# Feed-forward input projection by seven block products instead of eight, with block sums made on chip

## The reference

```python
    x = x + gt1 * (merged @ w_out)
    h2 = rmsnorm(x, g_norm[1]) * (1 + sc2) + sh2
    u, gg = jnp.split(h2 @ w_ffn_in, 2, axis=-1)
    x = x + gt2 * ((jax.nn.silu(gg) * u) @ w_ffn_out)
```

## Time and profile before

| what | value |
|---|---|
| median of 3 runs | 1094.04 us (1091.89 to 1094.91) |
| profiled execution, first to last instruction | 1095.1 us |
| PE busy | 1045.0 us (95%) |
| DVE, ACT, POOL busy | 395.5, 366.5, 368.7 us |
| feed-forward input stage, about | 676 to 948 us |

### The profile page before, as it was taken

The page is one execution under the profiler, slowest core; times in us unless marked ns, Lnnn a source line. Parts: engine busy times, 40 slices in busy tenths (PEclk is TensorE's granted clock), DMA queues, the critical chain, the costliest instruction groups (busy, mean ns, idle before and its releaser), DMA issues.

```text
span 1095.1 us, 25416 instructions
## 1 busy us (share of the span) xinstructions
PE 1045.0 (95%) x10988; PEld 966.9 (88%) x10988; DVE 395.5 (36%) x926; ACT 366.5 (33%) x745; POOL 368.7 (34%) x252
## 2 busy tenths in 40 slices
PE   6999999999998988989898999999999999999997
PEld 3899989999996766777787999999999999999997
DVE  4400000194045676566556576222222222200003
ACT  4443333353444444345232233322322232211112
POOL 2165433343316061401160333333343334344331
PEclk8899999999999999899998999999999999999999
DMA  9986666343311000020341532233222322132322
GB/s 358 352 276 235 234 206 198 99 139 119 113 42 36 18 7 22 13 82 3 131 130 43 198 116 58 77 92 99 77 77 83 107 78 65 55 104 79 92 67 82
DMA packets 118174, 122.23 MB, mean 112 GB/s; under 512 B 5396, under 2 KB 102848, under 8 KB 115656
## 3 DMA queue, kind: packets, MB, share of 16 engines
q1 hardware_dynamic: 112864, 111.86, 31.8%
q10 hardware_dynamic: 5224, 9.10, 2.5%
HBM read 108.33 MB, written 15.23 MB: 113 GB/s over the span
## 4 chain that ended last, share of the span: by engine, by line
PE 86%; DVE 7%; issue 3%; ACT 3%; POOL 1%; ACTq 1%; DVEq 0%; POOLq 0%
PE ps L1566 83%; PE ps L1917 2%; DVE s_sb L1306 1%; PE ps L1817 1%; POOL w_lo L595 1%; DVE s_sb L1340 1%; ACT x_sq L743 0%; DVE xn L1118 0%; DVE gring L1477 0%; DVE Pb L1277 0%; DVE y_sb L1549 0%; DVE mt L1479 0%; ACT mgh L1031 0%; DVE XX L1287 0%; ACTq L729 0%
## 5 line engine op out<-in xcount | busy, mean ns | idle before, releaser
L595 POOL TENSOR_TENSOR w_lo<-w_raw,w_hi 128x2048 fp32r<-128x2048 f32 (+1 forms) x66 | 282.3, 4277 | 564.0 <-ACT w_hi L753 544.9
L1566 PE MATMUL ps<-hh,w_hi 128*128 128x274 f32 x1376 | 290.0, 293 | 2.7 <-DVE hl L1128 2.0
L1566 PE MATMUL ps<-hh,w_lo 128*128 128x274 f32 x1376 | 288.1, 292 | 0.0
L1566 PE MATMUL ps<-hl,w_hi 128*128 128x274 f32 x1376 | 286.6, 291 | 0.0
L1566 PEld LDWEIGHTS ps<-hh,w_hi 128*128 128x128 f32 x1376 | 219.0, 190 | 12.8 <-issue 11.2
L1566 PEld LDWEIGHTS ps<-hh,w_lo 128*128 128x128 f32 x1376 | 218.7, 190 | 0.8 <-issue 0.8
L1566 PEld LDWEIGHTS ps<-hl,w_hi 128*128 128x128 f32 x1376 | 219.0, 190 | 0.0
L753 ACT ACTIVATE w_hi<-w_raw 128x2048 fp32r<-128x2048 f32 (+1 forms) x66 | 117.5, 1781 | 106.6 <-PE ps L1566 101.1
L1566 PE MATMUL ps<-ah,w_hi 128*128 128x274 f32 x352 | 75.3, 290 | 0.3 <-POOL w_lo L595 0.3
L1566 PE MATMUL ps<-ah,w_lo 128*128 128x274 f32 x352 | 75.4, 290 | 0.0
L1566 PE MATMUL ps<-al,w_hi 128*128 128x274 f32 x352 | 75.2, 290 | 0.0
(11 more groups left out here) (375 smaller groups left out, 1537.8 us busy)
## 6 DMA issues: line engine op xcount, KB each, us to landing
w_raw<-in_w_ffn_in SPq DMA_DIRECT2D x44, 512.0 KB, 4.6
w_raw<-in_w_in SPq DMA_DIRECT2D x42, 512.0 KB, 5.0
ada_l<-in_w_ada SPq DMA_DIRECT2D x16, 1024.0 KB, 6.4
ada_w<-in_w_ada SPq DMA_DIRECT2D x8, 1024.0 KB, 13.6
w_raw<-in_w_ffn_out SPq DMA_DIRECT2D x16, 384.0 KB, 4.0
w_raw<-in_w_ffn_out SPq DMA_DIRECT2D x16, 320.0 KB, 3.4
g_d<-gst SPq DMA_DIRECT2D x16, 274.0 KB, 2.4
gring<-g_d SPq DMA_DIRECT2D x16, 274.0 KB, 3.2
```

The costliest lines, as they stand in the source:

```text
L595: pool.tensor_tensor(w_lo[:, s, 0:cols], w_raw[:, s, 0:cols], w_hi[:, s, 0:cols].bitcast(F32), ALU.subtract).then_inc(lo_done, 1)
L1566: return pe.matmul(out, lhsT, rhs, start=start, stop=stop)
```

## The change

The first unit (U_UP) stays as it was. For the other 21 the unit is one 2 x 2 block product: rows are the gate's (A11, A12) and the up block (A21, A22) with even and odd k blocks as columns of A; B11, B12 are the two halves of the tokens for even k, B21, B22 for odd k. The Winograd form of Strassen's scheme makes it with seven products of 4 k blocks x 3 terms = 12 matmuls, 84 for a unit.

- Token sums t1 to t4 (`tq`, float32), 4 subtractions of 274 columns for each of the 4 pairs of k blocks, are made once on DVE in the loop of the output projection's residuals; ACT makes their high parts `th`, POOL their low parts `tl`, each in 4 operations of 4 x 274 columns.
- Weight sums s1 to s4 (`w_sum`, one buffer, 4 x 512 columns) are made for every unit on DVE.
- ACT and POOL make high and low parts of 7 x 512 columns a unit in 4 groups (1024, 1024, 512, 1024 columns), into one buffer `ws_hi`, `ws_lo`: a group is overwritten when its products of the unit before are done.
- A unit takes four PSUM banks, two sets in turn. Products 3, 5 and 6 are added to banks whose content ACT has copied before (`rest`, 4 copies of 274 columns); DVE adds bank and copy for each of the four quarters, then scales by `rstd2` (both operands in SBUF now).
- The activations are kept in float32 (`a_f`). Their high parts go to the memory of `hh`, `hl`, `th`, `tl` as these come free in the last unit; ACT makes them and DVE the low parts at the end of the stage (`act_high`, `act_low`), and PE's first output tile waits block by block.
- `w_raw` holds the two blocks one behind the other. Final norm buffers move.

```diff
-            two_by_two(sp, U_UP, NUP, up)
+            def up_later(i, s):
+                sp.wait_ge(wslo_done, i * NGR + (WSLO - (U_ST + 1) * NGR))
+                up_blocks(i, s)
...
+            def token_low(c):
+                pool.wait_ge(th_done, TH + c + 1)
+                pool.tensor_tensor(tl[:, :, c, :], tq[:, c % 2, :, :], th[:, :, c, :].bitcast(F32), ALU.subtract)\
+                    .then_inc(tl_done, 1)
...
+            def blocks_low(i, s):
+                for g, (a, z) in enumerate(FIRST_OF):
+                    pool.wait_ge(wshi_done, i * NGR + (WSHI + g + 1 - U_ST * NGR))
+                    of = blocks(a, z)
+                    pool.tensor_tensor(of(ws_lo), group_source(s, g), of(ws_hi).bitcast(F32), ALU.subtract)                        .then_inc(wslo_done, 1)
+            two_by_two(pool, U_ST, NST, blocks_low)
...
+            def blocks_high(i, s, g):
+                a, z = FIRST_OF[g]
+                if g in (0, 2):
+                    act.wait_ge(raw_in[s], i * 16 + (32 - 16 * s))
+                else:
+                    act.wait_ge(wsum_done, i * 4 + (WSUM + (3, 4)[g // 2] - U_ST * 4))
+                if isinstance(i, int) and i == U_ST:
+                    act.wait_ge(unit_mm, U_UP + (g >= 2))
+                else:
+                    act.wait_ge(prod_mm, i * NPR + (PROD + z - (U_ST + 1) * NPR))
+                act.activation(blocks(a, z)(ws_hi), group_source(s, g), ACT.Copy).then_inc(wshi_done, 1)
...
+            def up(i, s):
+                kept(i, s, 0)
+                blocks_high(i + 1, 1 - s, 0)
+                kept(i, s, 1)
+                kept(i, s, 2)
+                blocks_high(i + 1, 1 - s, 1)
+                kept(i, s, 3)
+                blocks_high(i + 1, 1 - s, 2)
+                gated_silu(i)
+                blocks_high(i + 1, 1 - s, 3)
...
+            def token_sums(c):
+                if c >= 2:
+                    dve.wait_ge(tl_done, TL + c - 1)
+                b11, b12, b21, b22 = [tmp_a[:, r, h * H:(h + 1) * H] for r in range(2) for h in range(2)]
+                t1, t2, t4, t3 = [tq[:, c % 2, b, :] for b in range(4)]
+                tt(t1, b12, b11, ALU.subtract).then_inc(tq_done, 1)
+                tt(t3, b12, b22, ALU.subtract).then_inc(tq_done, 1)
...
+                if j:
+                    token_sums(i)
...
+            def weight_sums(i, s):
+                dve.wait_ge(raw_in[s], i * 16 + (32 - 16 * s))
+                if not (isinstance(i, int) and i == U_ST):
+                    dve.wait_ge(wslo_done, i * NGR + (WSLO - U_ST * NGR))
+                a11, a12, a21, a22 = [raw_block(s, m, j) for m in range(2) for j in range(2)]
+                s1, s2, s4, s3 = [w_sum[:, b, :].rearrange("p (c m) -> p c m", m=P) for b in range(4)]
+                tt(s3, a21, a11, ALU.subtract).then_inc(wsum_done, 1)
+                tt(s1, a21, a22, ALU.add).then_inc(wsum_done, 1)
+                dve.wait_ge(wsum_done, i * 4 + (WSUM + 1 - U_ST * 4))
+                tt(s2, s3, a22, ALU.add).then_inc(wsum_done, 1)
+                dve.wait_ge(wsum_done, i * 4 + (WSUM + 3 - U_ST * 4))
+                tt(s4, a12, s2, ALU.subtract).then_inc(wsum_done, 1)
...
+            def quarter(i, s, n):
+                out, p, r, b = ((ff_g[:, 0:H], 1, 0, 1), (ff_g[:, H:W], 5, 2, 2), (ff_a[:, H:W], 6, 1, 0),
+                                (ff_a[:, 0:H], 6, 3, 0))[n]
+                dve.wait_ge(rest_ev, i * 4 + (REST + (1, 3, 2, 4)[n] - U_ST * 4))
+                dve.wait_ge(prod_mm, i * NPR + (PROD + p + 1 - U_ST * NPR))
+                tt(out, ps[:, 4 * (1 - s) + b, 0:H], rest[:, r, :], ALU.add).then_inc(quad_ev, 1)
+
+            def gate_up(i, s, between):
+                dve.wait_ge(act_f32, i - U_UP)
+                quarter(i, s, 0)
+                between()
+                quarter(i, s, 1)
+                dve.wait_ge(quad_ev, i * 4 + (QUAD + 10 - U_ST * 4))
+                tt(ff_g[:, :], ff_g[:, :], rstd2[:, :], ALU.mult).then_inc(ffg_f32, 1)
+                quarter(i, s, 2)
+                quarter(i, s, 3)
+                dve.wait_ge(quad_ev, i * 4 + (QUAD + 12 - U_ST * 4))
+                tt(ff_a[:, :], ff_a[:, :], rstd2[:, :], ALU.mult).then_inc(ffa_f32, 1)
+                dve.wait_ge(ffa_f32, i + (FFA + 1 - U_ST))
+                activated(i)
...
+            gate_up(U_DN - 1, (U_DN - 1) % 2, first_low)
+            for c in range(6, FT):
+                act_low(c)
...
+            def seven(i, s):
...
+                for p, (b, x) in enumerate(((0, b11), (1, b21), (2, t1), (0, t2), (3, t4), (2, b22), (0, t3))):
+                    if p in (0, 2, 4, 5):
+                        pe.wait_ge(wslo_done, i * NGR + (WSLO + GROUP_OF[p] + 1 - U_ST * NGR))
+                    if p == 0:
+                        pe.wait_ge(quad_ev, i * 4 + (QUAD + 4 - U_ST * 4))
+                    fresh = p in (0, 1, 2, 4)
+                    if not fresh:
+                        pe.wait_ge(rest_ev, i * 4 + (REST + {3: 1, 5: 2, 6: 3}[p] - U_ST * 4))
+                    xh, xl = x
+                    for c in range(HK):
+                        w = slice(block_column(p, c), block_column(p, c) + P)
+                        for j, (wt, xt) in enumerate(((ws_hi, xh), (ws_hi, xl), (ws_lo, xh))):
+                            ins = pe.matmul(ps[:, 4 * (1 - s) + b, 0:H], wt[:, w], xt[c], start=fresh and c == 0 and j == 0,
+                                            stop=c == HK - 1 and j == 2, skip_group_check=not fresh)
+                    ins.then_inc(prod_mm, 1)
```

More of the change, by code:

```diff
@@ L304, in build @@
         T_UP = T_WO + 2 * NWO
[L305 removed]
+        T_DN = T_UP
         T_Y = T_DN + KD
@@ L1066, in _, with kept @@
-            down = lambda i, s: high(i + 1, 1 - s, KDN * P)
+            def kept(i, s, which):
+                p, b = ((0, 0), (2, 2), (3, 0), (4, 3))[which]
+                act.wait_ge(prod_mm, i * NPR + (PROD + p + 1 - U_ST * NPR))
+                if which == 1 and not (isinstance(i, int) and i == U_ST):
+                    act.wait_ge(quad_ev, i * 4 + (QUAD + 8 - U_ST * 4))
+                act.activation(rest[:, which, :], ps[:, 4 * (1 - s) + b, 0:H], ACT.Copy).then_inc(rest_ev, 1)
+            blocks_high(U_ST, U_ST % 2, 1)
@@ new lines, in _ @@
+            gated_silu(U_UP)
+            for g in (2, 3):
+                blocks_high(U_ST, U_ST % 2, g)
+            def up(i, s):
[8 more added lines that the diff above has]
+                blocks_high(i + 1, 1 - s, 3)
+            up(U_ST, U_ST % 2)
@@ new lines, in act_high @@
+            def act_high(c):
+                act.wait_ge(prod_mm, PROD + LAST + (1 if c < KD else 3 if c < 12 else 4 if c < 14 else 6))
+                act.wait_ge(act_f32, c + 1)
+                act.activation(act_hi(c), a_f[:, c, :], ACT.Copy).then_inc(ah_done, 1)
+            i, s = U_DN - 1, (U_DN - 1) % 2
+            kept(i, s, 0)
+            for c in range(4):
+                act_high(c)
+            kept(i, s, 1)
+            down_high(U_DN, U_DN % 2)
+            kept(i, s, 2)
+            act_high(4)
@@ L1534, in _ @@
+            gate_up(U_DN - 1, (U_DN - 1) % 2, first_low)
+            for c in range(6, FT):
+                act_low(c)
+            for k in range(2):
+                dve.wait_ge(unit_mm, U_DN - NST + 2 * k + 2)
+                residual(k, k, GT2).then_inc(pair_free, 1)
+            with link.loop(KD // 2 - 2, 4) as k2:
                 for j in range(2):
-                    dve.wait_ge(unit_mm, k2 * 4 + (U_DN + 2 * j + 2))
-                    residual(j, k2 * 2 + j, GT2).then_inc(pair_free, 1)
@@ L2151, in down_tile @@
-                    x = [(c * P, ah[:, part_ * KDN + c, :], al[:, part_ * KDN + c, :]) for c in range(KDN)]
-                    product(k + T_DN, j, (U_DN + part_) % 2, x, part_ == 0, part_ == 1).then_inc(unit_mm, 1)
-            with pe.Fori(0, KD // 2 - 1) as k2:
+                    product(k + T_DN, j, part_, down_terms(part_), part_ == 0, part_ == 1).then_inc(unit_mm, 1)
+            pe.wait_ge(quad_ev, QUAD + 4 * NST + 4)
+            for part_ in range(2):
+                pe.wait_ge(lo_done, U_DN - NST + part_ + 1)
+                for c, term in enumerate(down_terms(part_)):
+                    pe.wait_ge(act_done, part_ * KDN + c + 1)
+                    ins = product(T_DN, 0, part_, [term], part_ == 0 and c == 0, part_ == 1 and c == KDN - 1)
+                ins.then_inc(unit_mm, 1)
@@ L2154, in _ @@
+            down_tile(1, 1)
+            with pe.Fori(1, KD // 2 - 1) as k2:
                 for j in range(2):
@@ L2164, in turn @@
                 return ins
-            u, n = U_DN + 2 * KD - 2, T_DN + KD - 1
+            u, n = U_DN - NST + 2 * KD - 2, T_DN + KD - 1
             pe.wait_ge(lo_done, u + 1)
-            product(n, 1, U_DN % 2, [(c * P, ah[:, c, :], al[:, c, :]) for c in range(KDN)], True, False).then_inc(unit_mm, 1)
+            product(n, 1, 0, down_terms(0), True, False).then_inc(unit_mm, 1)
             pe.wait_ge(lo_done, u + 2)
```

199 lines of the change are left out of this document (144 added, 55 removed).

## The result

The kernel with the change takes 1117.88 us, the median of 4 runs (1114.62 to 1119.57), against 1094.33 for the kernel before in the same comparison: a ratio of 1.0208, 95% interval 1.0185 to 1.0231. The forecast was 1119.5. The profiled executions have spans of 1114.3 and 1095.1 us; the 19.2 us between them are what has to be found in the traces.

The account below looks back on a forecast made before the run. The mutual exclusion of VectorE and GpSimd was taken as the bound: +19 for the units, +5 entrance, +1.5 exit, +25.5 on the profiled 1095.1 us, 1120.6, hence a median of 1119.5; range 1100 to 1142.

Parts of the forecast that it names:

- the lock: Units: GpSimd and two-SBUF-input VectorE instructions exclude each other whole; 13.7 us of such work against 10.74 a unit.
- the signs named: Units: low parts at 2.4 and 1.27 us, TensorE idle 2 us or more, stretched scalings and first sum, quarters at 0.43.
- rival D: Units: TensorE's clock falls too; about 14.1 us a unit, 1133 to 1150 us in all; chance 0.12.
- TensorE stays the bound: Units: GpSimd and VectorE interleave without queueing; 10.74 us a unit, 1066 us in all; chance 0.07.
- 13.2: Length in us forecast for one of the 21 changed units, likely span 12.8 to 13.6.
- the ring: Units: closed cycle of GpSimd, VectorE and ScalarE steps, each waiting for the one before; sum 13.3 us.
- the hand-over: Units: a change of owner between GpSimd and VectorE hides 0.14 to 0.15 us of the next instruction's start.
- another order of the two: Units: the two scalings placed in a different order in the cycle, which then sums to 13.0 us.
- Twenty-one units: +19: Units: 21 x (13.2 - 12.3) = +19 us, between +10 and +27.
- Entrance, +5: Output projection into first unit: late last residual makes TensorE stand 4 us, first weight sums 1 late; 0 to +9.
- exit, +1.5: After the last unit: TensorE waits for VectorE's low parts of the activations; +1.5 us, between 0 and +4.
- A hand-over hides nothing: Units: seven changes of owner cost 1.0 us more; 14.3 us a unit, 1142 us in all; chance 0.04.

Follow-up runs that it names:

- e3: On e2, three of the four weight sums take one input from ScalarE's copy in PSUM instead of SBUF: 1084.85 us, ratio 0.9904.
- e4: On e3, the quarters are summed in place in PSUM and the two scalings read PSUM: 1076.08 us, ratio 0.9838.
- e5: On e4, the first output tile takes high-part terms first; some ScalarE splits and six VectorE low parts come earlier: 1072.1 us, ratio 0.9795.
- e8: On e5, VectorE makes the next tile's residual earlier, and the first weight sums read PSUM and precede the reciprocal: 1064.47 us, ratio 0.9722.
- e7: On e4, e5's edit plus the first unit in free PSUM pairs and first weight sums, from SBUF, before the reciprocal: 1075.39 us, ratio 0.9835.
- e9: On e8, the scalings of the eight tiles move from VectorE to ScalarE: 1065.29 us, ratio 0.9721.
- e1: Changed kernel with product 1 of every unit cut to one of its four k blocks, 3 matmuls instead of 12: 1115.47 us.
- e2: Changed kernel with ScalarE copying the up block into idle PSUM banks, the weight sums still reading SBUF: 1115.77 us, ratio 1.0182.

## Why the prediction was right, and where it wasn't

**The bound.** The forecast, that the lock takes TensorE's place, held. Of the signs named, these are in the rows: quarters at 0.43, the up half's scaling and the first sum ending 0.57 and 0.54 behind a low part, TensorE at 84 matmuls a unit and waiting for GpSimd. Others came out otherwise: only group 0's low part kept its 2.40 us, the three that wait for VectorE took 1.8 to 2.9; the gate's scaling was never held (729 ns); TensorE's pause was 1.76 and not 2 or more, and stood before product 2 alone, not also at group 3. The clock below 1, the sign of rival D, showed too (0.96), but cost nothing here. e3 and e4 show the cause, not only the coincidence: with one input moved to PSUM (and in e4 the waits that go with it), the unit goes from 12.73 to 11.12 to 10.69. The rival "TensorE stays the bound" was worked out at 1066 and failed on its condition alone; when e4, e5 and e8 removed what stood against it, the kernel took 1064.5.

**The unit, mis-sized: 13.2, measured 12.72.** Three terms of the ring, which summed to 13.27, were too long. Pause, product and third low part (0.12 + 0.75 + 2.24 = 3.11) were 2.81, from the end of one low part at 813.68 to that of the next at 816.49: the wait for the semaphore passed while GpSimd was at work, and the hand-over hid 0.19 of the product. The gate's scaling, put at 0.59, came ahead of its low part and held it for 0.44. The sums and ScalarE's part were 3.00 instead of 3.12. That is 0.30 + 0.15 + 0.12 = 0.57, and the other steps together were 0.02 longer than forecast. The order differed in one point: both scalings came a place earlier, the gate's ahead of group 1's low part and the up half's ahead of group 2's. (The forecast had priced another order of the two at 13.0.)

**Twenty-one units: +19, measured +5.1.** 21 x (12.72 - 12.30) is 8.8, not 19: 10 of the 13.9 us of error are the mis-sized unit. The other 3.7 us: the first interval between two Silus is 11.31, where the ring has yet to close, and the last product doesn't wait for a next unit's sums. A steady rate was multiplied by a count that includes both ends.

**Entrance, +5, measured +8.4; exit, +1.5, measured +7.3.** The entrance's mechanism was the one described, the last residuals behind three groups of token sums and three blocked scalings (680 forecast, 679.78 measured). The step that failed is that the price ended with the pause. The half clock after it, 2.7 us here and 2.2 at the exit, was weighed for the units, from the earlier trace rows, where slack absorbs it, and not for the transitions, where nothing does. At the exit the bounds (0 to +4) failed too: I looked at VectorE's lead from the last product on, and the six low parts placed ahead of that were not free but held the quarters back. The seventh was begun 7.0 us behind the last product, not 5.5 to 6, and was then itself held (4.36 for two).

**"A hand-over hides nothing", 14.3 a unit.** The rows have it otherwise: every blocked instruction ended sooner after its release than it would have taken alone (0.57 for 0.73, 0.54 for 0.69), some 0.15 us. The Trainium skill's sentence in "SBUF — State Buffer", "Who interferes with whom", that the other engine is blocked for the whole instruction holds for the order; for a sum of many short steps these 0.15 us count.

So the time was hit by luck in part: 14 us too much in the units and 9 too little in the transitions largely cancelled, and of the 6 that are left against the traces (25.5 forecast, 19.2 found) another 4.4 vanish because the profiled executions lie closer together than the medians (23.6 apart).

## What to carry to other kernels

If work is moved from TensorE to VectorE and GpSimd, don't add their busy times; write down which VectorE instructions have two SBUF inputs, put them and GpSimd's instructions one behind the other in the order that the semaphores force, and compare that ring with TensorE's time. One input in PSUM takes an instruction out of the ring (here 1115.8 to 1084.9 to 1076.1 us). Price a transition by its pause plus some half-clock time behind it (here 0 to 2.7 us for one transition). When a pause only moves on being removed, look first whether the edit itself put something into the ring, then at the order on the engine that feeds it, and only then at its load.

## What the runs showed of the hardware

Blocked VectorE and GpSimd instructions take strict turns, one for one, as long as both have a next one queued: the 32-column product, 0.25 us of work, takes 2.35 to 2.40 us in 20 of the 22 units, and GpSimd, which has low parts queued, doesn't run two in a row past it: in the unit shown it ends 0.06 us behind one low part, and the next low part ends 2.30 behind it. TENSOR_SCALAR, with one tensor and a column of scalars in SBUF, was held as long as a two-tensor instruction (4.49 us for 32 columns), while scalings that read PSUM never were (718 to 732 ns in the kernel before, e4, e5 and e7 to e9). And with one pause of 1.76 us in most units, the granted clock fell to half for 3.4 us five times in the 21 units of the changed kernel, at no cost, since TensorE had the slack.

The same pause doesn't always bring the same time at half clock. With the entrance's pause of 5.3 us it was 6.8 us in the changed kernel, e1 and e3, and 3.4 in e2, e4 and e5. A pause of 1.96 us in an output tile of e5 was followed by none, one of 1.95 in e7 by 3.4.

What stays open: how the entrance's loss divides between the token sums (four times 0.44 us for each pair of tiles) and the held scalings. e8 removes it with nothing taken off VectorE, e9 shows that with that order the held scalings don't matter, and no kernel in which only one of the two is taken from the old order was run.
